# Where the modulation rows of a diffusion trunk are summed: 28 of 48 chunks from TensorE to VectorE and GpSimd

## The reference, cut to what matters

```python
sc, scc = silu(c), silu(c_ctx)                    # two vectors of 1024
for l in range(2):
    mod_x = sc  @ w_mod[l] + b_mod[l]             # w_mod[l] is 1024 x 6144
    mod_c = scc @ w_mod[l] + b_mod[l]
    sh1, sc1, g1, sh2, sc2, g2 = split(mod, 6)    # for x and for ctx
    h = x * (1 + sc1) + sh1                       # the same for ctx
    x = layernorm(ALPHA * x + g1 * mixer(h))      # mixer: attention
    h = x * (1 + sc2) + sh2
    x = layernorm(ALPHA * x + g2 * ffn(h))        # layer 0: SwiGLU, layer 1: 2 of 8 experts
```

## Time and profile before

| what | us |
|---|---|
| median of the runs | 1804.23 (1804.13 to 1807.76, 3 runs) |
| span of the profiled execution, first to last instruction | 1800.0 |
| difference of the two (the execution has no time of its own outside its span) | 4.2 |
| TensorE busy | 1663.3 (92%) |
| VectorE busy | 744.5 (41%) |
| ScalarE busy | 620.8 (34%) |
| GpSimd busy | 31.3 (2%) |
| mean granted TensorE clock | 0.981 |

### The profile page before, as it was taken

The page is one execution under the profiler, slowest core; times in us unless marked ns, Lnnn a source line. Parts: engine busy times, 40 slices in busy tenths (PEclk is TensorE's granted clock), DMA queues, the critical chain, the costliest instruction groups (busy, mean ns, idle before and its releaser), DMA issues.

```text
span 1800.0 us, 26541 instructions
## 1 busy us (share of the span) xinstructions
PE 1663.3 (92%) x10786; PEld 1203.7 (67%) x10786; DVE 744.5 (41%) x1147; ACT 620.8 (34%) x904; POOL 31.3 (2%) x50
## 2 busy tenths in 40 slices
PE   5999989899999999999879998888899998998897
PEld 3885558788888777876657666665566666665554
DVE  2434655433323355744754222223443323222447
ACT  2325662423222334324733322223333222232332
POOL 1200000000000000000010000000000000000000
PEclk8999999999999999999979999999999999999999
DMA  9825753223223544320249999999999999999996
GB/s 348 202 96 191 301 188 117 71 94 117 94 83 117 209 153 165 117 91 27 80 161 372 417 421 420 421 420 410 419 409 388 421 420 421 421 420 410 420 418 243
DMA packets 112055, 481.96 MB, mean 268 GB/s; under 512 B 8218, under 2 KB 46280, under 8 KB 62784
## 3 DMA queue, kind: packets, MB, share of 16 engines
q1 hardware_dynamic: 109344, 472.66, 66.6%
q0 software_dynamic: 2592, 7.62, 1.8%
HBM read 477.38 MB, written 2.87 MB: 267 GB/s over the span
## 4 chain that ended last, share of the span: by engine, by line
PE 67%; DMA 16%; DVE 7%; ACT 5%; issue 3%; SPq 0%; DVEq 0%; ACTq 0%
PE PS L892 17%; PE PS L894 16%; PE PS L893 16%; DMA RAWA<-in_w_exp_up 11%; ACT BH L2109 3%; DMA RAWA<-in_w_exp_down 3%; PE PS L1581 3%; PE PS L919 2%; PE PS L1511 2%; DVE RAWAL L2908 2%; PE PS L1168 2%; DMA RAWB<-in_w_exp_down 1%; PE PS L1190 1%; PE PS L1178 1%; DMA RAW<-in_w_mod 1%
## 5 line engine op out<-in xcount | busy, mean ns | idle before, releaser
L2273 DVE TENSOR_TENSOR WL<-RAW,WH 128x2048 fp32r<-128x2048 f32 (+1 forms) x61 | 137.6, 2256 | 290.3 <-ACT WH L1754 290.1
L892 PE MATMUL PS<-HH,WH 128*128 128x512 f32 (+1 forms) x600 | 228.0, 380 | 10.2 <-DVE HL L2312 2.9
L894 PE MATMUL PS<-HH,WL 128*128 128x512 f32 (+1 forms) x600 | 224.8, 375 | 0.0
L893 PE MATMUL PS<-HL,WH 128*128 128x512 f32 (+1 forms) x600 | 224.6, 374 | 0.0
L1754 ACT ACTIVATE WH<-RAW 128x2048 fp32r<-128x2048 f32 (+1 forms) x61 | 115.2, 1888 | 287.0 <-PE PS L894 287.0
L2908 DVE TENSOR_TENSOR RAWAL<-RAWA,BH 128x2048 fp32r<-128x2048 f32 x44 | 100.9, 2292 | 268.1 <-ACT BH L2109 268.1
L892 PE MATMUL PS<-BH,HE 128*128 128x512 f32 x448 | 181.5, 405 | 12.0 <-DVE RAWAL L2908 10.4
L2908 DVE TENSOR_TENSOR RAWBL<-RAWB,BH 128x2048 fp32r<-128x2048 f32 x39 | 89.4, 2292 | 217.7 <-ACT BH L2109 217.7
L894 PE MATMUL PS<-BH,LE 128*128 128x512 f32 x448 | 175.5, 392 | 0.0
L2109 ACT ACTIVATE BH<-RAWA 128x2048 fp32r<-128x2048 f32 x44 | 84.2, 1913 | 243.5 <-DMA RAWA<-in_w_exp_up 157.6
L2109 ACT ACTIVATE BH<-RAWB 128x2048 fp32r<-128x2048 f32 x39 | 74.6, 1914 | 236.1 <-DMA RAWB<-in_w_exp_up 154.7
(11 more groups left out here) (363 smaller groups left out, 2564.0 us busy)
## 6 DMA issues: line engine op xcount, KB each, us to landing
RAWB<-in_w_exp_up SPq DMA_DIRECT2D x112, 1024.0 KB, 10.5
RAWA<-in_w_exp_up SPq DMA_DIRECT2D x112, 1024.0 KB, 10.8
RAWA<-in_w_exp_down SPq DMA_DIRECT2D x56, 1024.0 KB, 10.3
RAWB<-in_w_exp_down SPq DMA_DIRECT2D x56, 1024.0 KB, 9.8
RAW<-in_w_mod SPq DMA_DIRECT2D x48, 1024.0 KB, 6.1
RAW<-in_w_ffn_up SPq DMA_DIRECT2D x22, 1024.0 KB, 5.1
RAW<-in_w_in_c SPq DMA_DIRECT2D x12, 1024.0 KB, 5.2
RAW<-in_w_ffn_down SPq DMA_DIRECT2D x10, 1024.0 KB, 5.1
```

Of the source, the lines that this page charges most:

```text
L892: mm(ps, ah, bh, start=start, stop=False)
L893: mm(ps, ah, bl, start=False, stop=False)
L894: return mm(ps, al, bh, start=False, stop=stop)
L2273: v.tensor_tensor(WL[:, c % 2, 0:n], raw("weight", c)[:, 0:n], WH[:, c % 2, 0:n].bitcast(F32), ALU.subtract).then_inc(s_lo, 1)
```

## The change

Chunks are dealt out anew: units 0 and 1 at the start as before; units 2 to 4 (12 chunks) in attention 0, one chunk in each of the groups 0 to 11; units 5 to 9 (20 chunks) in FFN up, one for each of its 22 weight chunks except the ninth and the last; units 10 and 11 (8 chunks) in FFN down, one at each step from the first. So 16 chunks leave attention and 4 leave FFN down's share.

The 28 chunks of units 5 to 11 are no longer multiplied on TensorE. The latents' row is accumulated by VectorE, the context's by GpSimd, each as an elementwise product of the weight tile with one column of ST held in all its 1024 columns, in a tile MSUM[:, row, :] of 128 partitions x 1024. GpSimd waits until VectorE has its part of a chunk, and a load into the slot waits for GpSimd. When all four chunks are in, `mod_sum` on TensorE sums over the partitions: 8 matmuls with a selector (PICK) as weights. Rows and columns go on as before. In FFN up the sums stand at the start of stages 4, 6, 8 and 10, the columns 24 matmuls later. The fold of a LayerNorm's rows into the modulation of layer 1 moves from the end of attention 0 to stage 7 on VectorE.

```diff
-MOD_PRE, MOD_ATT, MOD_DOWN = 2, 7, 2
-MOD_LAST = MOD_PRE + MOD_ATT + MOD_DOWN
+MOD_PRE, MOD_ATT, MOD_UP, MOD_DOWN = 2, 3, 5, 2
+MOD_PE = MOD_PRE + MOD_ATT
+MOD_LAST = MOD_UNITS - 1
...
+        def mod_at_stage(st):
+            return {4: MOD_PE, 6: MOD_PE + 1, 8: MOD_PE + 2, 10: MOD_PE + 3}.get(st)
+        def mod_half(n):
+            return n + (n >= 8)
...
-            chunks_here = {C_OUT0: MQ * MOD_ATT, C_DN + DU + 4: 2, C_DN + DU + 5: 2}
-            for _ in range(chunks_here.get(c, 2 * (C_DN + 2 < c <= C_DN + 2 + 2 * MOD_DOWN))):
+            chunks_here = {C_OUT0: MQ * MOD_ATT}
+            chunks_here.update({C_UP + mod_half(n) + 3: 1 for n in range(MQ * MOD_UP)})
+            chunks_here.update({C_DN + 2 + n: 1 for n in range(MQ * MOD_DOWN)})
+            for _ in range(chunks_here.get(c, 0)):
...
-                    sp.wait_ge(s_lo if before == "weight" else s_modused, cb + 1)
+                    if before == "weight":
+                        sp.wait_ge(s_lo, cb + 1)
+                    elif cb < MQ * MOD_PE:
+                        sp.wait_ge(s_modused, cb + 1)
+                    else:
+                        sp.wait_ge(s_modg, 4 * (cb - MQ * MOD_PE + 1))
...
+            def mod_products(u):                                   # GpSimd
+                acc = mod_sums(u)[:, 1, :]
+                for q in range(MQ):
+                    ...
+                    gp.wait_ge(s_modv, n + 1)
+                    if q == 0:
+                        gp.tensor_scalar(acc, w[0], c[0], None, ALU.mult).then_inc(s_modg, 2)
+                        gp.tensor_scalar(w[1], w[1], c[1], None, ALU.mult).then_inc(s_modg, 1)
+                    else:
+                        gp.tensor_scalar(w[0], w[0], c[0], None, ALU.mult).then_inc(s_modg, 1)
+                        gp.tensor_scalar(w[1], w[1], c[1], None, ALU.mult).then_inc(s_modg, 1)
+                        gp.wait_ge(s_modg, 4 * n + 1)
+                        gp.tensor_tensor(acc, acc, w[0], ALU.add).then_inc(s_modg, 1)
+                    gp.wait_ge(s_modg, 4 * n + 3)
+                    gp.tensor_tensor(acc, acc, w[1], ALU.add).then_inc(s_modg, 1)
...
+            def mod_sum(u):                                        # TensorE
+                pe.wait_ge(s_modv, MQ * (u - MOD_PE + 1))
+                pe.wait_ge(s_modg, 4 * MQ * (u - MOD_PE + 1))
+                for r in range(2):
+                    for j in range(4):
+                        last = mm(PS[j * LANE:(j + 1) * LANE, bank, at:at + 256], PICK[:, r, :],
+                                  mod_sums(u)[:, r, j * 256:(j + 1) * 256], start=(r == 0), stop=(r == 1))
+                last.then_inc(s_modsum, 1)
...
-                    if i < 2 * MOD_ATT:                            # TensorE, attention 0
-                        mod_chunk(MQ * MOD_PRE + 2 * i)
-                        mod_chunk(MQ * MOD_PRE + 2 * i + 1)
+                    if i < MQ * MOD_ATT:
+                        mod_chunk(MQ * MOD_PRE + i)
...
+                        u = mod_at_stage(st)                       # TensorE, FFN up
+                        if u is not None and gu == 0:
+                            mod_sum(u)
+                        if u is not None and gu == 1:
+                            pe.wait_ge(s_modc, u + 1)
                         for j in range(2):
+                            if u is not None and (gu, j) == (0, 1):
+                                mod_columns(u)
...
-                    if 1 <= i <= 2 * MOD_DOWN:                     # TensorE, FFN down
+                    if i == 2:
                         pe.wait_ge(s_gate, 8)
-                        for n in range(2):
-                            mod_chunk(MQ * (MOD_PRE + MOD_ATT) + 2 * (i - 1) + n)
-                    if i in (DU + 2, DU + 3):
-                        pe.wait_ge(s_yread, y_read[1] + 3)
-                        for n in range(2):
-                            mod_chunk(MQ * MOD_LAST + 2 * (i - DU - 2) + n)
+                        mod_sum(MOD_PE + MOD_UP - 1)
+                    if i == DU + 3:
+                        pe.wait_ge(s_yread, y_read[1] + 4)
+                        mod_sum(MOD_LAST - 1)
+                        mod_sum(MOD_LAST)
...
+                if mod_at_stage(st + 1) is not None:               # ScalarE, FFN up, ahead of split(cg + 4)
+                    mod_row_out(mod_at_stage(st + 1))
...
+                dve.wait_ge(*landed("mod", m))                     # VectorE, mod_products(n)
+                if q == 0:
+                    link(v.tensor_scalar(acc, w[0], c[0], None, ALU.mult))
+                else:
+                    link(v.scalar_tensor_tensor(acc, w[0], c[0], acc, ALU.mult, ALU.add))
+                v.scalar_tensor_tensor(acc, w[1], c[1], acc, ALU.mult, ALU.add).then_inc(s_modv, 1)
...
                     if j == 1:                                     # VectorE, FFN up
+                        if mod_at_stage(st + 1) is not None:
+                            mod_columns(mod_at_stage(st + 1))
+                            if st + 1 == 8:
+                                dve.wait_ge(s_modc, 8)
+                                fold(1, 0, 1).then_inc(s_fold, 1)
+                        if 2 * st in mod_halves:
+                            mod_products(mod_halves[2 * st])
                         split(cg + 4)
...
+                if 2 * st + 1 in mod_halves:
+                    mod_products(mod_halves[2 * st + 1])
...
+            mod_products(MQ * MOD_UP)                              # VectorE, FFN down
             for i in range(len(units)):
                 split(min(C_DN + i + 3, C_IN1 + 1))
                 if i + 2 < len(units):
                     product_lo(i + 2)
+                if i + 1 < MQ * MOD_DOWN:
+                    mod_products(MQ * MOD_UP + i + 1)
```

More of the change, by code:

```diff
@@ L207, in trunk @@
         TMP = sb("TMP", [P, 512], F32, R0 + 80 * K)
+        MSUM = [sb(f"MSUM{i}", [P, 2, D], F32, at) for i, at in
+                enumerate((R0 + 52 * K, R0 + 64 * K, R0 + 72 * K, 32 * K, 40 * K))]
         WR = sb("WR", [P, KT, LANE], F32, 113 * K)
@@ L554, in trunk @@
         NG0 = len(groups[0])
-        assert 2 * MOD_ATT <= NG0 - 2 and MOD_LAST + 1 == MOD_UNITS
+        assert MQ * MOD_ATT <= NG0 - 2 and MOD_PE + MOD_UP + MOD_DOWN == MOD_UNITS
         g_base = [0, NG0]
@@ L837, in _ @@
             gp.memset(ST[:, :, 2:LANE], 0.0).then_inc(s_stz, 1)
+            gp.memset(PICK[:, :, :], 0.0).then_inc(s_pick, 1)
+            gp.wait_ge(s_pick, 1)
+            for r in range(2):
+                gp.memset(PICK[:, r, r:r + 1], 1.0).then_inc(s_pick, 1)
             gp.dma_start(SINK[:, :], sink_a[0].partition_broadcast(P)).then_inc(s_small, 16)
@@ L859, in _ @@
                         .then_inc(s_bl, 16)
-            for p in range(3):
+            def mod_products(u):
+                acc = mod_sums(u)[:, 1, :]
+                for q in range(MQ):
+                    m = MQ * u + q
+                    n = m - MQ * MOD_PE
+                    w = [raw("mod", m)[:, k * D:(k + 1) * D] for k in range(2)]
+                    c = [ST[:, 2 * q + k, 1:2] for k in range(2)]
+                    gp.wait_ge(s_modv, n + 1)
[9 more added lines that the diff above has]
+                    gp.tensor_tensor(acc, acc, w[1], ALU.add).then_inc(s_modg, 1)
+            for p in range(3):
+                if p == 1:
+                    for u in range(MOD_PE, MOD_PE + MOD_UP):
+                        mod_products(u)
+                    gp.wait_ge(s_modsum, MOD_UP)
+                if p == 2:
+                    for u in range(MOD_PE + MOD_UP, MOD_UNITS):
+                        mod_products(u)
                 if p % 2 == 0:
@@ L912, in mod_chunk @@
                 bank, at = mod_place(u)
-                if q == 0 and MOD_PRE < u < MOD_PRE + MOD_ATT:
+                if q == 0 and u > MOD_PRE:
                     pe.wait_ge(s_modrow, u)
@@ L2454, in attention0 @@
                     normalise(i)
[L2455 to L2456 removed]
+                    if i % MQ == 0 and MQ <= i <= MQ * MOD_ATT:
+                        mod_columns(MOD_PRE + i // MQ - 1)
                     if i >= 1:
@@ L2459, in attention0 @@
                 block_lo(NG0 - 1)
-                dve.wait_ge(s_modc, MOD_PRE + MOD_ATT)
-                fold(0, 3, 0)
-                fold(1, 0, 1).then_inc(s_fold, 1)
+                dve.wait_ge(s_modc, MOD_PE)
+                fold(0, 3, 0).then_inc(s_fold, 1)
             def attention1():
@@ L2672, in product_lo, with mod_products @@
                                 ALU.subtract).then_inc(s_gl, 1)
+            def mod_products(n):
+                u, q = divmod(n + MQ * MOD_PE, MQ)
+                acc = mod_sums(u)[:, 0, :]
+                m = n + MQ * MOD_PE
+                w = [raw("mod", m)[:, k * D:(k + 1) * D] for k in range(2)]
+                c = [ST[:, 2 * q + k, 0:1] for k in range(2)]
+                dve.wait_ge(*landed("mod", m))
+                if q == 0 and u - MOD_PE in (3, 4):
```

(11 more changed lines are left out.)

60 lines of the change are left out of this document (39 added, 21 removed).

## The result

The changed kernel takes 1869.83 us (median of 4 runs, 1866.02 to 1873.88) against 1804.66 for the kernel before on the same chip: ratio 1.0361, 95% interval 1.0348 to 1.0375. The forecast was 1811.4, in a range of 1792 to 1824. The direction was right; the size was far outside the range. The profiled execution spans 1867.6 us, 67.6 more than before.

What follows compares the result with a forecast made beforehand. TensorE was taken to bound the kernel. Its -10.8 us (with +0.5 and +0.7 undisturbed: -9.6) plus 6 and 12 for turns summed to +7.2: 1807.2 in the span, 1811.4 as a time, range 1792 to 1824.

Steps and rivals of the forecast that it cites:

- working bound on the multiply: GpSimd's multiply of one 128x1024 tile: between 1.11 us (from a memset) and the add's 2.35; 1.11 was taken.
- both ends (6.9 and 9.4) are below the 10.88: GpSimd's us per chunk at either multiply price, against TensorE's 10.88 per weight chunk: each engine is covered, one at a time.
- I charge nothing: SP's load queue: with 6.9 to 9.4 us a chunk on GpSimd, the buffer slot is free in time, cost 0.
- the likeliest case: VectorE operations with two SBUF inputs and GpSimd reads take turns, durations add: 6 plus 12 us; chance 0.41.
- FFN up, charged 6: Turns in FFN up: GpSimd adds delay VectorE's splits in four stages, 0 to 9 us, 6 taken.
- FFN down, charged 12: Turns in FFN down: 110.6 us asked for in 96.5 before the last sums; 9.8 to 14.1 too much, 12 taken.
- Costed at nothing: Several waits priced at 0, among them GpSimd's second LayerNorm row loads waiting for the fifth sum, some 16 us into FFN down.
- slow multiply with turns: Rival: GpSimd's multiply takes 2.35 us, not 1.11; 69 us more shared time, at least half showing, above 1845; chance 0.06.
- Attention, -7.6: Attention of layer 0: 16.4 us leave TensorE, but ScalarE is close behind, so 7.6 us gained; bounds 5 to 10.
- undisturbed sum, -9.6: Whole kernel without turns: TensorE alone -10.8, waits before sums +0.5, FFN down's short unit +0.7, in us.
- 5.2 + 0.5: FFN up: four sums and four pairs of columns add 5.2 us on TensorE; VectorE's waits before sums about 0.5.
- -8.4 + 0.7: FFN down: 12 chunks leave and three sums come, -8.4 us on TensorE; VectorE late around the short unit, +0.7.

Runs made afterwards that it cites:

- the probe: Kernel before, plus 20 GpSimd instructions on unused 128x1024 tiles before attention begins; GpSimd's multiply by a scalar from SBUF took 2.85 us, no kernel time given.
- Thirteen fills: Changed kernel with GpSimd's four operations per chunk replaced by thirteen 128x1024 fills that read nothing: 1866.47 us, ratio 1.0335.
- eleven fills: Changed kernel with GpSimd's four operations per chunk replaced by eleven 128x1024 fills that read nothing: 1830.66 us, ratio 1.0140.
- the short multiplies: Changed kernel with GpSimd's multiplies on 384 of the 1024 columns, the rest not multiplied: 1833.21 us, ratio 1.0157.
- Eight fills: Changed kernel with GpSimd's four operations per chunk replaced by eight 128x1024 fills that read nothing: 1808.0 us, ratio 1.0007.

## Why the prediction was wrong

*The working bound on the multiply failed.* "From above the add's 2.35" was a guess dressed as a bound: nothing says that one tile read costs no more than two. Alone it takes 2.85. Four instructions alone are 2 x 2.85 + 2 x 2.40 = 10.5 us, not 6.9, and 8.1 in a unit's first chunk: 9.9 on average, 10.2 with the gaps of 0.09 between the probe's instructions. That is still under the step of 10.88.

*The step that decided it:* "both ends (6.9 and 9.4) are below the 10.88", and "beyond 10.9 a chunk it would cost the excess every step". The condition was right and I never let the turns act on it. I counted turns as lateness of VectorE's splits; but GpSimd's own instructions wait too, and carry its chunk from 9.9 to 12.5, over the step. So the wait for a free buffer, "I charge nothing", was the term that failed. Thirteen fills, with that much GpSimd time and no turns with splits, products or multiply-adds, bring 60 us over the run without GpSimd's work, of the 64 to 65. The changed kernel's chunk of 12.5 (its gaps add next to nothing: the last eight chunks span 100.2 us, 99.5 of them busy) lies between the 11.4 and 13.4 of the fills; an estimate along the line between them gives some 44 us for pace, and the other 20 then belong to VectorE's longer instructions. That division is worked out, not shown by a run, and rough, since the changed kernel's chunks are uneven (9.5 and 13.5) and the fills' are not.

*The limit in FFN down.* I compared GpSimd with the step of 10.88 and, in the sum for FFN down, gave it the whole stretch from 574.3. It can't begin unit 10 before the fifth sum, 16 us in by my own text, since its row loads stand ahead and wait for it. What is left is 9.6 us a chunk, and eleven fills, which read nothing, already cost 24 us there.

*The turns themselves.* Right as a mechanism, and the likeliest case was theirs. I charged 18 us; the short multiplies, whose 9.2 a chunk stay below the step on the mean, cost 28 over no GpSimd arithmetic. Eight fills (8.3) cost next to nothing and eleven (11.4) 24, so on the line between them pace could account for some 7 of the 28. In FFN down it may be more: there eight chunks took 81.3 us (608.05 to 689.4), 10.2 each, which on the line between the fills is some 16 of the 25. How much is turns as such and how much their effect on the pace isn't settled. FFN up, charged 6, took 6.4 in that run (315.2 us from gates to gates, against 308.8); FFN down, charged 12, took 25 (153.5 against 128.6).

*"Costed at nothing": GpSimd's row loads.* I asked who reads the rows and not who stands behind them in the queue. Unit 10's products do: 7 us undisturbed, 8 in the changed kernel.

*The rival "slow multiply with turns", above 1845,* named the time that came, and half of the reason. Its multiply of 2.35 was still too cheap, and it priced 69 us more of shared time; it has no word of the pace, which thirteen fills show to bring most of the loss. It had a chance of 0.06 since I put the multiply at the low end of bounds that were themselves too low.

*Attention, -7.6.* Measured -6.1 (270.1 to 264.0), within 5 to 10. From attention's first scores to its gates it is 121.9 us in the kernel before and 114.3 to 117.6 in the ten traces that have the new attention: 4.3 to 7.6 less, so a difference of one or two from my term means little. The wait of ScalarE's copies fell by 6.9:

```profile
  PE PS L1251: 6.3, 18
```

for 13.2 in the earlier trace rows, and ScalarE has no idle time ahead of its first copies in most groups, as predicted. In this trace the clock then took some back: in the window 240 to 260 TensorE is busy for 15.09 us instead of 18.64, its granted clock is 0.91 instead of 1.00, and one group takes 9.57 us (copies at 245.40 and 254.97) where it took 7.96; in it 32 matmuls at L1263 take 3.06 us (granted clock 0.66 from 247 to 252) where the next 32 take 1.97 at 1.00:

```profile
240.00:260.00 20.00, 15.09 (x146) 11.11 (x144) 12.29 (x51) 11.55 (x29) 0.00 (x0) 0.91 0.00 1
```

*The undisturbed sum, -9.6.* With nobody waiting for GpSimd the median is 6.9 less by the ratio, and 3.6 by the span. By the events: attention -4.5, FFN up +7.1 (I had 5.2 + 0.5), FFN down -6.5 (I had -8.4 + 0.7). No term is out by much more than 3. The 0.5 for the waits ahead of sums didn't show: TensorE is busy for 239.9 of the 240 us from 330 to 570 in that run. From the first split to the last, FFN up is 6.5 longer (235.0 for 228.5), so a sum with its columns cost 1.6 and not 1.3.

## What to carry to other kernels

When work is moved to an idle engine, first take its instruction by itself on the chip: neither a cheaper-looking nor a similar one bounds it. Then ask for its pace with all that it must take turns with, against every limit of what waits for it: at 8.3 us a chunk it was free within the noise, at 11.4 it cost 3.3 us in FFN up, where 10.88 is the limit, and 24.3 in FFN down, where it had 9.6 a chunk. And when a wait is put into a queue, list what stands behind it there, not only who reads what the waiting instruction makes. Here one engine doing both rows, and only for the units that sat on TensorE's path, was faster than two engines sharing them.

## What the runs showed of the hardware

- GpSimd on 128x1024 alone: multiply by a scalar from SBUF 2.85 us, by a constant 2.77, add or product of two tiles 2.40, copy 1.04, fill 0.95. A multiply of one tile costs nearly three copies; I had expected a fill's price.
- A GpSimd multiply reads one tile and still takes turns: 4.82 at 464.88 and 7.00 at 646.16 in the changed kernel, for 2.84 undisturbed. Even the copy did, once: 2.98 beside a split.
- Fills take no turns with VectorE's operations of two SBUF inputs: 364 of them at a mean of 962 ns, with multiply-adds at 1281.
- VectorE's multiply of one tile by a scalar, which I put at 0.75 us, is 0.75 on the mean in the four runs where GpSimd is idle, 1.24 in the changed kernel, and 1.10 in the run of eleven fills (1.62 at 537.87). So it, alone of these forms, is delayed by an engine that only writes; why isn't settled.
